# A weight chunk's low half moved from VectorE to GpSimd, its high half earlier on ScalarE

## What is computed

```python
h_lat = h_lat + g2 * swiglu(modulate(rms_norm(h_lat, norm_ffn_g[i]), sh2, sc2), ...)
h_ctx = h_ctx + cg2 * swiglu(modulate(rms_norm(h_ctx, norm_ffn_g[i]), csh2, csc2), ...)
...
a_lat = modulate(rms_norm(h_lat, norm_mix_g[i]), sh1, sc1)
a_ctx = modulate(rms_norm(h_ctx, norm_mix_g[i]), csh1, csc1)
...
proj = h @ (w_in if with_q else w_in[:, MLA_Q_LORA:])      # w_in: 768 + 256 + 32 columns
q_lat, kv_lat, k_pe = proj[..., :768], proj[..., 768:1024], proj[..., 1024:]
```

## Time and profile before

| | before |
|---|---|
| three runs | 1349.55, 1350.08, 1353.41 us |
| median | 1350.08 us |
| the profiled execution's own time | 1350.16 us |
| its span (first to last instruction) | 1348.0 us |
| mean granted clock of TensorE | 0.995 |
| TensorE matmul busy | 1297.4 us, 96% |
| VectorE busy | 876.8 us, 65% |
| ScalarE busy | 543.3 us, 40% |
| GpSimd busy | 26.0 us, 2% |
| DMA | 218.79 MB, mean 162 GB/s |

### The profile page before, as it was taken

How to read it: one execution, slowest core, us unless ns; L and a number is a source line. 1 busy time by engine, 2 the same in 40 slices (tenths; PEclk the granted TensorE clock), 3 DMA queues, 4 the chain that set the end, 5 groups by cost and what they waited for, 6 DMA issues and landing times.

```text
span 1348.0 us, 16642 instructions
## 1 busy us (share of the span) xinstructions
PE 1297.4 (96%) x6780; PEld 1057.2 (78%) x6780; DVE 876.8 (65%) x1221; ACT 543.3 (40%) x734; POOL 26.0 (2%) x60
## 2 busy tenths in 40 slices
PE   7999999999899999999999999999899989899998
PEld 6888777887777787878787878887876667888887
DVE  5777676568654455666565646535777786767777
ACT  5465453464421122432222213133476665554442
POOL 0000000000000000000000000000021110000000
PEclk9999999999999999999999999999999999999999
DMA  9525477734554532365454554322131221355551
GB/s 356 208 94 203 172 269 261 256 150 172 203 187 187 219 125 69 120 248 197 179 195 180 186 189 165 147 72 74 41 116 64 83 106 63 125 188 187 187 187 63
DMA packets 24359, 218.79 MB, mean 162 GB/s; under 512 B 3168, under 2 KB 8288, under 8 KB 11360
## 3 DMA queue, kind: packets, MB, share of 16 engines
q1 hardware_dynamic: 22432, 212.21, 42.5%
q0 software_dynamic: 864, 3.15, 0.7%
q10 hardware_dynamic: 992, 2.44, 0.5%
HBM read 216.74 MB, written 1.05 MB: 162 GB/s over the span
## 4 chain that ended last, share of the span: by engine, by line
PE 77%; DVE 12%; ACT 6%; issue 3%; DMA 2%; SPq 0%; DVEq 0%; ACTq 0%
PE bank L597 20%; PE bank L599 19%; PE bank L598 19%; PE bank L609 6%; DVE w_lo L1863 4%; PE bank L610 3%; PE turned L625 2%; ACT w_hi L1313 2%; PE mod_ps L646 2%; PE bank L1114 2%; DVE scaled L1904 2%; DMA raw<-in_mlp 1%; DVE h L2195 1%; DMA raw<-in_w_in 1%; DVE gated L2288 1%
## 5 line engine op out<-in xcount | busy, mean ns | idle before, releaser
L1863 DVE TENSOR_TENSOR w_lo<-raw,w_hi 128x2048 fp32r<-128x2048 f32 (+5 forms) x166 | 333.9, 2051 | 80.5 <-ACT w_hi L1313 80.4
L1313 ACT ACTIVATE w_hi<-raw 128x2048 fp32r<-128x2048 f32 (+5 forms) x166 | 276.6, 1714 | 184.9 <-PE bank L599 155.6
L597 PE MATMUL bank<-act_parts,w_hi 128*128 128x512 f32 (+1 forms) x600 | 225.0, 375 | 1.8 <-DVE act_parts L1888 1.8
L599 PE MATMUL bank<-act_parts,w_lo 128*128 128x512 f32 (+1 forms) x600 | 222.3, 371 | 0.0
L598 PE MATMUL bank<-act_parts,w_hi 128*128 128x512 f32 (+1 forms) x600 | 222.3, 370 | 0.0
L609 PE MATMUL bank<-act_parts,w_hi 128*128 128x512 f32 x544 | 192.0, 397 | 4.1 <-DVE silu L2195 1.4
L597 PE MATMUL bank<-w_hi,h_hi 128*128 128x512 f32 x392 | 154.7, 395 | 3.8 <-DVE h_lo L2210 3.0
L599 PE MATMUL bank<-w_hi,h_lo 128*128 128x512 f32 x392 | 152.7, 390 | 0.0
L598 PE MATMUL bank<-w_lo,h_hi 128*128 128x512 f32 x392 | 152.7, 390 | 0.0
L610 PE MATMUL bank<-act_parts,w_lo 128*128 128x256 f32 x544 | 152.3, 280 | 0.0
L597 PEld LDWEIGHTS bank<-act_parts,w_hi 128*128 128x128 f32 x600 | 113.8, 190 | 28.1 <-issue 7.4
(11 more groups left out here) (308 smaller groups left out, 1669.3 us busy)
## 6 DMA issues: line engine op xcount, KB each, us to landing
raw<-in_ffn SPq DMA_DIRECT2D x35, 2048.0 KB, 7.9
raw<-in_mlp SPq DMA_DIRECT2D x24, 2048.0 KB, 8.0
raw<-in_mod_gate SPq DMA_DIRECT2D x7, 2048.0 KB, 8.6
raw<-in_conv_in SPq DMA_DIRECT2D x8, 1536.0 KB, 7.4
raw<-in_w_gates SPq DMA_DIRECT2D x4, 2048.0 KB, 8.5
raw<-in_w_branch SPq DMA_DIRECT2D x4, 2048.0 KB, 8.0
raw<-in_mla_q SPq DMA_DIRECT2D x4, 1152.0 KB, 5.2
raw<-in_w_out SPq DMA_DIRECT2D x2, 2048.0 KB, 8.0
```

What stands on the lines that cost most here:

```text
L597: te.matmul(dst, sh, mh, start=(j == 0), stop=False)
L599: last = te.matmul(dst, sl, mh, start=False, stop=(j == len(terms) - 1))
L1313: act.activation(w_hi[:, s, part], raw[:, at % 2, part], ACT.Copy).then_inc(hi_ready, 1)
L1863: ve.tensor_tensor(w_lo[:, s, part], raw[:, at % 2, part], w_hi[:, s, part].bitcast(f32), ALU.subtract).then_inc(lo_ready, 1)
```

## The change

GpSimd gets two new instructions, `latent_low()`, between its fifth and sixth gate bias DMA. They subtract the two halves of chunk 0, 1408 elements a partition each, once the low half of the chunk before is there and the high half of this one. VectorE only counts this chunk, and waits for it before it subtracts the next one. ScalarE copies the high half of chunk 0 before the normalised rows of block 2 instead of after the high parts of block 2.

```diff
@@ gpsimd
             pool.wait_ge(x_ready, 8)
             gate_bias(2, (0,))
+
+            def latent_low():
+                c = [k for k, i in enumerate(WEIGHT_AT) if STREAM[i][0] == "mla_in"][1] + 1
+                s, at = (c - 1) % 2, WEIGHT_AT[c - 1]
+                pool.wait_ge(lo_ready, 2 * c - 2)
+                for half, (first, end) in enumerate(halves_of(KT * MLA_W)):
+                    pool.wait_ge(hi_ready, 2 * c - 1 + half)
+                    pool.tensor_tensor(w_lo[:, s, first:end], raw[:, at % 2, first:end], w_hi[:, s, first:end].bitcast(f32),
+                                       ALU.subtract).then_inc(lo_ready, 1)
+
+            latent_low()
             pool.wait_ge(x_ready, 10)
             gate_bias(3, (1,))
@@ scalar, norm_both
                 high(1)
+                if ahead:
+                    split(KT * MLA_W)
                 act.wait_ge(tr_done, n.at("tr"))
                 rows_out(xn[:, 0, :], res(2), 2)
...
                 scaled_hi([act_dst(act_hi, 1, half, 0) for half in range(2)])
-                if ahead:
-                    split(KT * MLA_W)
                 scaled_hi([act_dst(act_hi, 1, half, 1) for half in range(2)])
@@ vector, norm_both
                     if ahead and t == 0:
-                        split(KT * MLA_W)
+                        n.step("split")
@@ vector, after the latent rows of all blocks
+            ve.wait_ge(lo_ready, 2 * n.at("split"))
             split(KT * MLA_W)
```

## The result

The changed kernel takes 1354.27 us (median of 20 runs, 1350.95 to 1358.83), the kernel before 1350.08 us (20 runs, 1347.16 to 1353.41). The ratio is 1.0029 with a 95% interval of 1.0021 to 1.0038: 3.9 us slower, 2.8 to 5.1. The forecast was 3.3 us slower.

What follows compares the result with a forecast made beforehand. TensorE, with matmuls filling 96% of the span, was taken as the bound. −3.5 (gaps closed) + 5.1 (sums kept waiting) + 1.7 (clock fall) = +3.3 us, from the median 1353.4 us; range 1348.0 to 1356.0.

Steps and rivals of the forecast that it cites:

- The bound: TensorE idles before chunk 0 and before block 2, both from VectorE's subtraction; removing it gives −3.5 us.
- the collision: GpSimd's two halves meet VectorE's two residual sums of block 3 on SBUF, delaying the second sum: +5.1 us.
- GpSimd's time: Each half of chunk 0, 1408 elements, takes GpSimd 3.2 us to subtract.
- Who comes first: At block 3's first residual sum, GpSimd starts 0.15 us ahead of VectorE and gets SBUF first.
- the likeliest case: GpSimd first at block 3's residual sums, with a clock fall: +3.3 us, 1353.4 us, chance 0.45.
- Turns of a whole instruction: With SBUF operands, VectorE and GpSimd alternate whole instructions; block 3's sums take some 3.6 and 3.0 us.
- The clock: TensorE stands 5.2 us before its transposes, so its granted clock falls from 2.4 to 1.2 GHz: +1.7 us.
- What costs nothing: ScalarE's earlier copy, GpSimd's earlier `ISA` row, the later sixth bias DMA and VectorE's new wait: nothing.
- VectorE first: VectorE's first residual sum of block 3 beats GpSimd: +2.2 instead of +5.1 us; 1348.8 or 1350.5 us; chance 0.25.
- Slow GpSimd: GpSimd's subtraction takes 4.5 us a half, second sum of block 3 +7.7 us: 1356.0 us, chance 0.10.
- sharing: Engines share SBUF at block 3's sums, each taking twice its 0.69 us: 1348.0 us; chance 0.08 including no disturbance.
- the case in which the clock holds: GpSimd first at block 3's sums, but TensorE's clock stays up: +1.6 us, 1351.7 us, chance 0.12.

Runs made afterwards that it cites:

- e5: Changed kernel, but GpSimd fills chunk 0's low half with zeros instead of subtracting: 3.1 us faster than the kernel before (interval 1.6 to 4.6).
- e6: Changed kernel with TensorE's order altered, needed products filling its wait: 4.3 us slower than the kernel before (2.8 to 5.9).
- e8: The changed kernel measured again, unaltered: 4.7 us slower than the kernel before (3.0 to 6.5).
- e9: Changed kernel with TensorE computing block 1's product a second time during its wait: median 1352.37 us, 3.0 us slower than the kernel before (1.2 to 4.7).
- e10: Changed kernel, but GpSimd copies raw to the low half, reading one SBUF operand instead of two: 0.0 us against the kernel before (−1.6 to 1.6).
- e1: Kernel before with only ScalarE's copy of chunk 0 moved early, VectorE still subtracting: 2.0 us faster (0.5 to 3.4).
- e7: Changed kernel, but GpSimd waits for the second half of ScalarE's copy before starting: 2.4 us slower than the kernel before (0.8 to 3.9).

## Why the prediction was right

- *The bound.* VectorE's subtraction held TensorE twice. Right: without it and without the collision the place is 3.7 us shorter (e5), forecast −3.5. The two gaps of the earlier trace rows are gone in the profile after.
- *GpSimd's time.* 3.2 us a half, from rows of 64 and 128 elements: 3.22 for the first in the profile after. The mean of the 256-element rows, 0.82 us, held waiting in it, as argued.
- *Who comes first.* GpSimd, as in the likeliest case, though by 0.06 us and not 0.15. The step from the end of the copy's first half to GpSimd's start is 0.16 us (945.20 to 945.36), where 0.08 was forecast. The four traces with this start (changed, e6, e8, e9) all have 0.06, so it repeats. But the step was mis-sized by more than the lead that was left: 0.07 us more and VectorE would have been first. That the side came out right owes something to luck.
- *Turns of a whole instruction.* Forecast 3.6 and 3.0 us for the sums, measured 3.71 and 2.92; the reciprocal 5.2 us later, forecast 5.1. No turn here had two waiting at once: the second sum begins at 949.76, when GpSimd's second half already has the access; that the longer waiter goes next is seen only in the earlier trace rows. The Trainium skill (SBUF — State Buffer, Who interferes with whom) says that a VectorE instruction with two SBUF inputs contends with a GpSimd instruction that reads SBUF, and not with one that only writes it. The runs agree, further than the forecast needed: one SBUF operand on GpSimd is enough (e10), none is not (e5), and VectorE's gate product, with an operand in PSUM, takes 0.68 us at 949.05 beside GpSimd.
- *The clock.* It fell, at the end of a gap of 5.38 us. Here is the term that was mis-sized: "A fall takes ... +1.7 us" took one fall as long as the one in the earlier trace rows, and this one lasted twice that, 3.4 us of deficit less the 0.6 to 1.0 that lie in the wait. Every fall in the kernel before had 1.7, so its trace gave no sign of the longer kind. The changed kernel's place is 2.6 us longer than e9's, in the second execution (e8) 21.26 − 19.03 = 2.2. So −3.7 + 5.2 + 2.6 is 4.1 where −3.5 + 5.1 + 1.7 was forecast.
- *What costs nothing.* The copy's move costs nothing (e1). The `ISA` row doesn't either: GpSimd's queue has two entries of line 498 besides the arithmetic, 37 ns each, at 932.9 us, 12 us before it. That the later bias DMA costs nothing was not tested by itself.

Rivals: VectorE first is what e7 makes. I had put its wait at 2.2 us with GpSimd beginning at the first sum's end; in e7 it begins 0.5 us later, and the wait is 2.9. Slow GpSimd is ruled out by its first half (3.22 us), sharing by the sums, and the case in which the clock holds by both traces of the changed kernel.

## What to carry to other kernels

Before work goes to an idle engine, list what the engine that shares its access to SBUF does in those microseconds: here each instruction of GpSimd that read SBUF delayed a VectorE instruction with two SBUF operands by up to nearly its own length (3.0 us by one of 3.2), and two such instructions in a row paid twice. Look first for idle time of the engine that already does the work: here 2.65 us stood open 7 us earlier, once ScalarE's copy came early too, and took both halves for 0.3 us. And price a new gap of TensorE with the slow stretch behind it, not by its length alone.

## What was new about the hardware

- Falls of the clock came in two sizes, a deficit of 1.7 us or of 3.4 us. The larger followed the gap of 5.38 us both times; the gap of 2.72 us at 1157 us was followed by either. Keeping TensorE on useless matmuls was cheaper at this place than leaving it idle (19.03 against 21.61 us).
- GpSimd's fill of 1408 elements takes 1.25 us (2.49 for two) and leaves VectorE's sums at 0.69 us. Its copy reads one operand, takes 3.13 us for two with VectorE's sum between, and makes them 1.83 and 1.13.
- A lead of 0.06 us decided over 3 us of waiting, in four traces of four.
